# Attention values of the last query tile with V as the stationary operand, in a one-core decoder block kernel

## The chip, the cores and the metric

The kernel runs on one core of one Trainium2 chip. The metric is the device time of one execution in microseconds (us); the time of a version is the median of its runs.

## The reference

One decoder block on x of 512 tokens by 1024 columns, all in float32:

```python
h = rmsnorm(x, ln_mix_g) * (1 + sc1) + sh1
(rq, rk, rv, rg, q, kc, vc, ks, vs, kw, vw, gate) = split(h @ w_in)
y_ret = retention(rope(rq), rope(rk), rv) * silu(rg)          # 4 heads, dk 64, dv 128
y_nsa = g0 * o_cmp + g1 * o_sel + g2 * o_win                  # 8 query heads, 2 groups, dh 64
x = x + ga1 * (concat(y_ret, y_nsa) @ w_out)
h2 = rmsnorm(x, ln_ffn_g) * (1 + sc2) + sh2
x = x + ga2 * ((silu(h2 @ w_gate) * (h2 @ w_up)) @ w_down)
return rmsnorm(x, ln_final_g)
```

With 512 tokens the selected branch takes all 8 blocks and the window covers everything before a query, so `o_sel` and `o_win` are each a causal softmax attention over up to 512 keys: `softmax(mask(q k^T / 8)) v`, with their own keys and values and the same queries. The change touches these two for the last 128 queries.

## The kernel before, in words

Each engine has a program of its own, written out by hand and joined by semaphores: the tensor engine (PE), the vector engine (DVE), the scalar engine (ACT), GpSimd (POOL) and the DMA queue of SyncE (SP). There are four token tiles of 128. Accuracy in the large products is had by splitting both sides into a high and a low part of type fp32r and adding three products; plain float32 products are used where the operands are not split, and PE executes such a product as two records of the profile.

**The attention loop.** A group x is (query tile i, branch b), x = 2i + b, so there are 8 groups; group x has i + 1 key tiles, which gives 20 steps (`STEP0` holds the first step of each group). Groups 6 and 7, steps 12 to 15 and 16 to 19, are the last query tile. Step n consists of

- `scores(n)` on PE: for both head groups g, the transposed scores of one key tile (128 keys on the partitions, 4 heads x 128 queries along the row) into PSUM banks 0 and 1, from four products of 64 rows each (lines 1343, 1345, 1347, 1350), plus the causal mask (line 1341 or 1355) where j = i. It waits until the exponentials of the step before are read out;
- `exp(n)` on ACT (line 610): 128x512 for each head group into `PT[:, n % 2]`, a buffer for two steps;
- `values(n)` on PE (line 1368): 8 plain float32 products, one per head, each with 128 columns of `PT` as the stationary operand and 65 columns of V moving. The 65th column of V is 1, so the sum of the weights falls out beside the output. It waits for exp(n), and it is issued one step late, behind scores(n + 1).

A loop over half steps (`SLOTS`, called slots below) places everything: slot 2n holds scores(n), slot 2n + 1 holds values(n - 1). Tables such as `PAIR_AT`, `RS_AT`, `RV_AT`, `CO_AT`, `M_AT` say behind which half the side work goes on every engine: `pair(x, h)` (line 1317), the raw scores from which DVE takes row minima with `row_min` (line 916); retention scores and values (lines 1411 and 1425), the decay multiply on DVE (line 984), the squares on ACT (line 620), the power on POOL (line 433); compressed attention (line 1400 and DVE line 973); `mix_transposes(i)` (line 1436), the transposes of a finished tile, behind `mix_high` on ACT and `mix_low` on DVE (line 1001).

Before a `pair` of query tile 3 or a retention score PE waits for everything that it issued earlier into banks 4 and 5:

```python
def maxima_free():
    for kind, s_ in (("pair", mx_min), ("block", mb_ok), ("decay", r_dec)):
        if issued[kind]:
            pe.wait_ge(s_, issued[kind])
```

When a group's values are done, DVE divides them by their sums and multiplies by the gate in `add_branch` (lines 935, 936, 939) and adds them to `mix` in `mix_branch` (line 947).

**The output projection.** `out_unit(t, k)` is six 128x512 products (lines 1232 to 1234) of token tile t and 128 rows of w_out, into banks 2t and 2t + 1. After the loop PE does four units (tiles 0 and 2, k = 0, 1), then mix_transposes(3), then twelve more for k < 4. Then it waits for the low parts of w_out rows k = 4 to 7, and does the last 16 units, tile by tile. DVE prepares those rows (scaling, line 849; low part, line 752, with ACT's high part, line 477, between) only after `mix_low(3)` in its program. SP reloads x and then the last w_out unit after the last scores, because x1 lies on the query buffers.

Of the kernel before, what the change touches and what calls it, by code (L numbers as in the profile page):

```python
# [7 lines left out]
F32 = mybir.dt.float32  # L8
# [42 lines left out]
GROUPS = 2 * TT  # L51
STEP0 = [0, 1, 2, 4, 6, 9, 12, 16, 20]
STEPS = STEP0[-1]
PAIR_AT = {1: [(4, 0)], 3: [(4, 1)], 6: [(4, 2)], 7: [(4, 3)], 10: [(5, 0)], 12: [(5, 1)], 13: [(5, 2)], 14: [(5, 3)], 15: [(6, 0)], 16: [(6, 1)], 19: [(6, 2)], 22: [(6, 3)], 24: [(7, 0)], 26: [(7, 1)], 29: [(7, 2)], 30: [(7, 3)]}
MAX_AT = {0: 2, 2: 3, 9: 4, 17: 5, 23: 6, 31: 7}
CS_AT = {9: 2, 21: 3}
CT_AT = {15: 2, 23: 3}
CO_AT = {0: 1, 16: 2, 25: 3}
RS_AT = {8: (1, 0), 11: (1, 1), 18: (2, 0), 21: (2, 1), 27: (3, 0), 28: (3, 1)}
RV_AT = {2: [(0, 0), (0, 1)], 10: [(1, 0)], 13: [(1, 1)], 20: [(2, 0)], 22: [(2, 1)], 29: [(3, 0)], 33: [(3, 1)]}  # L60
SQ_AT = {3: 0, 13: 1, 22: 2, 35: 3}
NORM_AT = {5: 0, 14: 1, 23: 2, 36: 3}
M_AT = {7: 0, 18: 1, 27: 2}
OUT_AT = {16: 0, 18: 1, 27: 2, 34: 3}
SLOTS = 2 * (STEPS + 1)
RAW = 7
EARLY = 8

# [39 lines left out]
def block_kernel(nc, x, c, ln_mix_g, ln_ffn_g, w_ada, b_ada, w_in, cmp_pe_k, cmp_w1_k, cmp_w2_k,  # L108
# [17 lines left out]
    with ExitStack() as ctx:  # L126
# [35 lines left out]
        QTl = at("QTl", [P, HPG, T], F32R, R + 8)  # L162
        KTh = at("KTh", [P, 2, T], F32R, R + 16)
        KTl = at("KTl", [P, 2, T], F32R, R + 20)
        V = at("V", [P, TT, 2, NG, DE], F32, R + 24)
        rqT = at("rqT", [P, 2, T], F32, R + 28.125)
        rkT = at("rkT", [P, 2, T], F32, R + 32.125)
# [17 lines left out]
        tmpo = at("tmpo", [P, T], F32, 107)  # L185
        sqj = at("sqj", [P, T], F32, 109)
        mcol = at("mcol", [P, 2, P], F32, 111)

        wxh = at("wxh", [P, OUT_TAIL, D], F32R, R + 16)
        wxl = at("wxl", [P, OUT_TAIL, D], F32R, R + 32)  # L190
# [25 lines left out]
        expo = small("expo", [P, TT])  # L216
        gates = small("gates", [P, TT, 3 * NH])
        rgt = small("rgt", [P, NH])
        mnc = small("mnc", [P, NH])
        yss = small("yss", [P, RH])  # L220
        hs = small("hs", [P, 2, 2 * CP])
# [121 lines left out]
        def _(sp):  # L343
# [32 lines left out]
            for kind, j in items:  # L376
                if kind == "early":
                    load_early(j)
                    continue
                if (kind, j) == ("w", 2):  # L380
                    sp.dma_start(cst[:, P:K_N], consts[:, P:K_N]).then_inc(const_in, 16)
                if kind == "w" and j in (9, 11):
                    sp.wait_ge(ada_used, ADA_OPS)
                    i = (j - 9) // 2
                    sp.dma_start(w1[:, i, :, :], (cmp_w1_k, cmp_w1_v)[i].rearrange("(j p) n -> p j n", p=P)).then_inc(w1_in, 16)
                if (kind, j) == ("w", 14):
                    sp.dma_start(masks[:, :], consts[:, K_N:K_N + T]).then_inc(masks_in, 16)
                if (kind, j) == ("w", U0_OUT):
                    sp.wait_ge(pairs_ps, 2 * NG)
                    sp.dma_start(decay[:, :, :], decays).then_inc(decay_in, 16)  # L390
                if (kind, j) == ("w", U0_GU + 38):
                    sp.wait_ge(mod_read, 10)
                    sp.dma_start(gfin[:, :], ln_final_g.partition_broadcast(P)).then_inc(gfin_in, 16)
                if (kind, j) == ("w", U0_GU - 1):

                    sp.wait_ge(st_ps, NG * STEPS)
                    sp.wait_ge(cs_ps, TT)
                    for t in range(TT):
                        sp.dma_start(x1[:, t, :], x[t * P:(t + 1) * P, :]).then_inc(xagain_in, 16)
                refill(ring.index((kind, j)))  # L400
# [8 lines left out]
        def _(pool):  # L409
# [31 lines left out]
            pool.dma_start(ga2[:, :], b_ada[5 * D:6 * D].partition_broadcast(P)).then_inc(bias2_in, 16)  # L441
            pool.wait_ge(mod_read, 7)
            pool.memset(mcol[:, :, :], 0.0).then_inc(mcol_set, 1)
            for i in range(TT):
                power(N_RET + i, yss[:, :])
            for u in range(U0_GU, UNITS):
                if u == U0_GU + SPLIT:
                    for t in range(TT):
# [7 lines left out]
        def _(a):  # L456
# [146 lines left out]
            def exp(n):  # L603
                for g in range(NG):
                    a.wait_ge(st_ps, NG * n + g + 1)
                    if n == 1:
                        a.wait_ge(r_y, 2)
                    if n >= 2:
                        a.wait_ge(pv, n - 1)
                    a.activation(PT[:, n % 2, g, :], ps[:, g, :], ACT.Exp, scale=-1.0).then_inc(p_exp, 1)  # L610

            def mix_high(i):
                a.wait_ge(mixT_ps, i + 1)
                a.activation(hTh[:, :, i * P:(i + 1) * P], ps[:, 6:8, :].rearrange("p b (k q) -> p (b k) q", k=4),
                             ACT.Copy).then_inc(mix_hi, 1)

            def ret_squares(i):
                a.wait_ge(r_y, 2 * (i + 1))
# [32 lines left out]
            cmp_copy(1)  # L651

            for n in range(SLOTS):
                if n % 2 == 0 and n // 2 < STEPS:
                    exp(n // 2)
                if n - 1 in CS_AT:
                    cmp_exp(CS_AT[n - 1])
                if n in CT_AT:
                    cmp_copy(CT_AT[n])
                if n in SQ_AT:  # L660
                    ret_squares(SQ_AT[n])
                if n in M_AT:
# [74 lines left out]
        def _(v_):  # L737
# [191 lines left out]
            def add_branch(x):  # L929

                i, b = divmod(x, 2)
                d.wait_ge(pv, STEP0[x + 1])
                o = ps[:, 2:4, 0:HPG * DE].rearrange("p g (h e) -> p g h e", e=DE)
                r = rgt[:, :].rearrange("p (g h) -> p g h", g=NG)
                then(d.reciprocal(r, o[:, :, :, DH]))
                then(d.tensor_tensor(rgt[:, :], rgt[:, :], gates[:, i, (b + 1) * NH:(b + 2) * NH], ALU.mult))
                if x:
                    d.wait_ge(b_mix, x)
                d.tensor_tensor(tmpo[:, :].rearrange("p (g h e) -> p g h e", g=NG, e=DH), o[:, :, :, 0:DH],
                                r.unsqueeze(3).broadcast_to([P, NG, HPG, DH]), ALU.mult).then_inc(o_read, 1)  # L940
            def mix_branch(x):

                i = x // 2
                d.wait_ge(o_read, x + 1)
                d.wait_ge(c_mix, i + 1)
                y = mix[:, i % 2, 512:1024]
                d.tensor_tensor(y, y, tmpo[:, :], ALU.add).then_inc(b_mix, 1)
                d.wait_ge(b_mix, x + 1)
# [125 lines left out]
            row_min(3, 3)  # L1074

            for n in range(SLOTS):
                if n % 2 and n // 2 in STEP0[1:]:
                    add_branch(STEP0.index(n // 2) - 1)
                for x, h in PAIR_AT.get(n, []):
                    row_min(x, h)  # L1080
                if n in MAX_AT:
                    max_rows(MAX_AT[n])
                if n % 2 and n // 2 in STEP0[1:]:
                    mix_branch(STEP0.index(n // 2) - 1)
                if n in CS_AT:
                    cmp_scores(CS_AT[n])
# [13 lines left out]
                    low(U0_OUT + OUT_AT[n - 1])  # L1100
                if n + 1 in OUT_AT:
                    scale_unit(U0_OUT + OUT_AT[n + 1])
            mix_low(TT - 1)

            def residual(t):
# [121 lines left out]
        def _(pe):  # L1227
# [129 lines left out]
            def values(n):  # L1357
# [11 lines left out]
                                 start=j == 0 and h == 0, stop=j == i and h == HPG - 1)  # L1369
                ins.then_inc(pv, 1)  # L1370

            def cmp_scores(i):
                if i == 0:
                    pe.wait_ge(kcT_lo, 1)
# [176 lines left out]
            for n in range(SLOTS):  # L1551
# [1 line left out]
                    scores(n // 2)  # L1553
                    half_rows(n)
                if n % 2 and n >= 3:
                    values(n // 2 - 1)
                if n in MAX_AT:
                    max_transpose(MAX_AT[n])
                if n in CS_AT:
# [23 lines left out]

            wait_low(pe, U0_OUT + 1)
            pe.wait_ge(mix_lo, TT - 1)
            pe.wait_ge(p_exp, NG * STEPS)
            pe.wait_ge(mb_ok, GROUPS)
            for k in range(2):  # L1590
                for t in (0, 2):
                    out_unit(t, k)
            mix_transposes(TT - 1)
            pe.wait_ge(o_read, GROUPS)
            out_unit(1, 0)
            out_unit(1, 1)
            pe.wait_ge(mix_lo, TT)
            for k in range(KT - OUT_TAIL):
                if k >= 2:
                    wait_low(pe, U0_OUT + k)  # L1600
                for t in range(TT) if k >= 2 else (TT - 1,):
                    ins = out_unit(t, k)
                ins.then_inc(unit_used, 1)

            def h2_transposes(t):
                pe.wait_ge(xb_ok, t + 1)
# [130 lines left out]
```

## Time and profile before

| | |
|---|---|
| median of 3 runs | 698.05 us (697.51 to 699.13) |
| profiled execution | 698.45 us, of which the span from first to last instruction is 696.6 us |
| PE busy | 671.5 us, 96% of the span |
| DVE, ACT, POOL busy | 334.2, 227.6, 187.8 us |
| attention steps and side work | about 185 to 279.5 us of the span |
| output projection up to its last 16 units | 279.5 to 302.3 us |

All times in rows are us from the start of the span unless marked ns. PE is busy nearly all the time, so what matters is how much time an instruction holds PE, and where PE would stand still. A matmul record's duration includes its pipeline, so the distance between the starts of two records tells how long one holds the engine.

### The profile page before, as it was taken

What the parts mean: (1) busy time and instruction counts of PE and PEld (TensorE: products, weight loads), DVE (VectorE), ACT (ScalarE), POOL (GpSimd) and SP (SyncE); (2) the same over time, 40 slices, a digit from 0 to 9 for tenths busy, and PEclk for the clock granted to TensorE, in tenths of its full rate; (3) what the DMA queues carried; (4) which work ended last, traced back from release to release, by engine and by line L of the source; (5) the groups of instructions that cost most, each with busy time, mean ns of one, the idle gap of its engine ahead of it and who ended that gap; (6) DMA issues with size and microseconds to landing.
All of it is one profiled execution on the core that took longest, in us unless ns stands there. A gap on an engine that the chain in (4) does not pass through costs nothing.

```text
span 696.6 us, 8985 instructions
## 1 busy us (share of the span) xinstructions
PE 671.5 (96%) x3571; PEld 560.8 (80%) x3571; DVE 334.2 (48%) x574; ACT 227.6 (33%) x384; POOL 187.8 (27%) x95
## 2 busy tenths in 40 slices
PE   2799999999999999999999999999999999999996
PEld 1699889887787878888988888888888888888885
DVE  4888988756577874626312531101000039533126
ACT  4546333250243434236432222222222122332224
POOL 2000000000000001050254445534444338455521
PEclk9899999999999999999999999999999999999998
DMA  9988967530000000870054545433432213231003
GB/s 309 362 277 309 384 226 278 208 121 32 0 2 1 1 1 30 248 206 1 3 158 143 152 144 157 121 91 90 121 118 95 91 60 121 95 111 68 0 1 121
DMA packets 74537, 88.08 MB, mean 126 GB/s; under 512 B 3112, under 2 KB 57600, under 8 KB 74368
## 3 DMA queue, kind: packets, MB, share of 16 engines
q1 hardware_dynamic: 73184, 85.31, 37.7%
q10 hardware_dynamic: 896, 1.12, 0.4%
q0 software_dynamic: 416, 1.08, 0.4%
q8 instruction: 28, 0.46, 0.3%
q14 instruction: 13, 0.11, 0.0%
HBM read 85.41 MB, written 2.10 MB: 126 GB/s over the span
## 4 chain that ended last, share of the span: by engine, by line
PE 93%; DVE 3%; issue 1%; DMA 1%; ACT 1%; SPq 0%; POOL 0%; POOLq 0%; DVEq 0%; ACTq 0%
PE ps L1232 14%; PE ps L1233 14%; PE ps L1234 14%; PE ps L1631 12%; PE ps L1632 12%; PE ps L1630 11%; PE ps L1368 5%; PE ps L1425 1%; PE ps L1317 1%; PE ps L1503 1%; DMA xs<-in_x 1%; PE ps L1343 1%; PE ps L1411 1%; PE ps L1245 1%; DVE acc L767 1%
## 5 line engine op out<-in xcount | busy, mean ns | idle before, releaser
L428 POOL TENSOR_TENSOR wl<-raw,wh 128x1024 fp32r<-128x1024 f32 x66 | 172.3, 2615 | 203.4 <-ACT wh L477 203.3
L1630 PE MATMUL ps<-hTh,wh 128*128 128x512 f32 (+1 forms) x384 | 143.6, 374 | 0.0
L1632 PE MATMUL ps<-hTh,wl 128*128 128x512 f32 (+1 forms) x384 | 142.6, 371 | 0.0
L1631 PE MATMUL ps<-hTl,wh 128*128 128x512 f32 (+1 forms) x384 | 142.6, 371 | 0.0
L477 ACT ACTIVATE wh<-raw 128x1024 fp32r<-128x1024 f32 x94 | 97.0, 1038 | 133.9 <-PE ps L1632 74.0
L1162 DVE TENSOR_TENSOR act<-ps,sg 128x512 f32<-128x512 f32 x22 | 15.2, 692 | 195.1 <-PE ps L1632 195.1
L1232 PE MATMUL ps<-wh,hTh 128*128 128x512 f32 (+2 forms) x232 | 90.2, 389 | 2.5 <-DVE hTl L821 2.5
L1233 PE MATMUL ps<-wl,hTh 128*128 128x512 f32 (+2 forms) x232 | 87.3, 376 | 0.0
L1234 PE MATMUL ps<-wh,hTl 128*128 128x512 f32 (+2 forms) x232 | 87.3, 376 | 0.0
L1630 PEld LDWEIGHTS ps<-hTh,wh 128*128 128x128 f32 x384 | 72.4, 188 | 13.0 <-issue 0.5
L1631 PEld LDWEIGHTS ps<-hTl,wh 128*128 128x128 f32 x384 | 72.4, 188 | 12.9 <-issue 0.5
L1632 PEld LDWEIGHTS ps<-hTh,wl 128*128 128x128 f32 x384 | 72.4, 188 | 12.3
L1232 PE MATMUL ps<-wh,ah 128*128 128x512 f32 x176 | 68.5, 389 | 0.0
L1233 PE MATMUL ps<-wl,ah 128*128 128x512 f32 x176 | 68.5, 389 | 0.0
L1234 PE MATMUL ps<-wh,al 128*128 128x512 f32 x176 | 68.5, 389 | 0.0
L1232 PEld LDWEIGHTS ps<-wh,hTh 128*128 128x128 f32 x232 | 44.4, 191 | 11.1 <-issue 3.1
L1157 DVE TENSOR_TENSOR al<-act,ah 128x512 fp32r<-128x512 f32 x22 | 28.3, 1288 | 50.5 <-ACT ah L701 50.5
L1234 PEld LDWEIGHTS ps<-wh,hTl 128*128 128x128 f32 x232 | 44.2, 191 | 8.0
L1233 PEld LDWEIGHTS ps<-wl,hTh 128*128 128x128 f32 x232 | 44.3, 191 | 7.3 <-issue 0.5
L849 DVE TENSOR_TENSOR raw<-raw,ga 128x1024 f32<-128x1024 f32 x30 | 44.8, 1511 | 0.0
L708 ACT ACTIVATE sg<-ps 128x512 f32<-128x512 f32 x22 | 13.2, 598 | 89.4 <-PE ps L1632 89.4
L433 POOL TENSOR_TENSOR yss<-yss,expo 128x4 f32<-128x4 f32 x4 | 5.0, 1242 | 135.9 <-DVE yss L990 135.9
(194 smaller groups left out, 867.4 us busy)
## 6 DMA issues: line engine op xcount, KB each, us to landing
raw<-in_w_ada SPq DMA_DIRECT2D x32, 512.0 KB, 5.4
raw<-in_w_ff_gate SPq DMA_DIRECT2D x22, 512.0 KB, 4.0
raw<-in_w_ff_up SPq DMA_DIRECT2D x22, 512.0 KB, 3.8
raw<-in_w_ff_down SPq DMA_DIRECT2D x22, 512.0 KB, 3.3
raw<-in_w_in SPq DMA_DIRECT2D x20, 512.0 KB, 7.6
early<-in_w_ada SPq DMA_DIRECT2D x16, 512.0 KB, 10.0
raw<-in_w_out SPq DMA_DIRECT2D x8, 512.0 KB, 3.7
xs<-in_x SPq DMA_DIRECT2D x4, 512.0 KB, 5.7
```

Of the source, the lines that this page charges most:

```text
L428: pool.tensor_tensor(lo, raw[:, slot, 0:n], hi.bitcast(F32), ALU.subtract).then_inc(w_lo2, 1)
L477: a.activation(split(u, n)[0], raw[:, slot, 0:n], ACT.Copy).then_inc(w_hi, 1)
L849: d.tensor_tensor(raw[:, slot, :], raw[:, slot, :], ga[:, :], ALU.mult).then_inc(w_scaled, 1)
L1157: d.tensor_tensor(al[:, f % SPLIT, :], act[:, f, :], ah[:, f % SPLIT, :].bitcast(F32), ALU.subtract).then_inc(a_lo, 1)
L1162: d.tensor_tensor(act[:, f, :], ps[:, 2 * (f % 2) + 1, :], sg[:, f % 2, :], ALU.mult).then_inc(act_ok, 1)
L1232: mm(o, ah_, bh_, start=first, stop=False)
L1233: mm(o, ah_, bl_, start=False, stop=False)
L1234: return mm(o, al_, bh_, start=False, stop=last)
L1368: ins = mm(ps[:, 2 + g, h * DE:(h + 1) * DE], PT[:, n % 2, g, h * P:(h + 1) * P], V[:, j, b, g, :], start=j == 0 and h == 0, stop=j == i a ...
L1630: mm(o, hi[:, ks], hTh[:, k, c0:c1], start=k == 0, stop=False)
L1631: mm(o, hi[:, ks], hTl[:, k, c0:c1], start=False, stop=False)
L1632: ins = mm(o, lo[:, ks], hTh[:, k, c0:c1], start=False, stop=k == KT - 1)
```

## The change

For groups 6 and 7 (steps 12 to 19) `values` is replaced by `wide_values`: V is the stationary operand (64 columns), the 512 weights of one head group move, and the two head groups write the two halves of the partitions of bank 2. The output is transposed (value columns on partitions), and V's column of ones is not used, so the sums of the weights are made apart: POOL adds the weights of a group's four steps in six additions (`weight_sum`), and after the loop PE sums them over the partitions with four products whose stationary operand is one column of ones (`den_sums`), which write partitions 0, 32, 64 and 96 of bank 3. ACT copies outputs and sums out of PSUM, PE transposes them back (8 + 4 transposes), DVE divides and adds (`den_gates`, `add_wide`). ACT's exp(n) now also waits for POOL where POOL still reads the buffer. More of the output projection (all of k < 4 for tiles 0 and 2) is done before mix_transposes(3). Some side work is in other slots. The reload of x waits for `den_sums`.

```diff
-PAIR_AT = {1: [(4, 0)], 3: [(4, 1)], ... 19: [(6, 2)], 22: [(6, 3)], 24: [(7, 0)], 26: [(7, 1)], 29: [(7, 2)], 30: [(7, 3)]}
+PAIR_AT = {1: [(4, 0)], 4: [(4, 1)], ... 20: [(6, 2)], 22: [(6, 3)], 24: [(7, 0)], 25: [(7, 1)], 29: [(7, 2), (7, 3)]}
-RV_AT = {2: [(0, 0), (0, 1)], 10: [(1, 0)], 13: [(1, 1)], 20: [(2, 0)], 22: [(2, 1)], 29: [(3, 0)], 33: [(3, 1)]}
-SQ_AT = {3: 0, 13: 1, 22: 2, 35: 3}
-NORM_AT = {5: 0, 14: 1, 23: 2, 36: 3}
+RV_AT = {2: [(0, 0), (0, 1)], 11: [(1, 0)], 13: [(1, 1)], 20: [(2, 0)], 22: [(2, 1)], 28: [(3, 0)], 34: [(3, 1)]}
+SQ_AT = {3: 0, 13: 1, 22: 2, 37: 3}
+NORM_AT = {5: 0, 14: 1, 23: 2, 38: 3}
+WIDE = GROUPS - 2
+WIDE0 = STEP0[WIDE]
+SUMMED = [n for x in (WIDE, WIDE + 1) for n in range(STEP0[x] + 1, STEP0[x + 1])]
+FILL = 4
...
# SP, before the reload of x
                     sp.wait_ge(cs_ps, TT)
+                    sp.wait_ge(den_ps, 1)
...
# POOL
-            for i in range(TT):
-                power(N_RET + i, yss[:, :])
+            def weight_sum(n):
+                x, j = step(n)
+                acc_ = sums(x % 2)
+                pool.wait_ge(p_exp, NG * (n + 1))
+                if j > 1:
+                    pool.wait_ge(p_sum, sum_count(n) - 1)
+                pool.tensor_tensor(acc_, weights(n - 1) if j == 1 else acc_, weights(n), ALU.add).then_inc(p_sum, 1)
+            for n in range(SLOTS):
+                if n - 1 in SQ_AT:
+                    power(N_RET + SQ_AT[n - 1], yss[:, :])
+                if n % 2 == 0 and n // 2 in SUMMED:
+                    weight_sum(n // 2)
...
# ACT, in exp(n)
+                    if n >= WIDE0 + 2:
+                        a.wait_ge(p_sum, sum_count(n - 2 if n - 2 in SUMMED else n - 1))
...
+            def out_copy(b):
+                a.wait_ge(pv, STEP0[WIDE + b + 1])
+                a.activation(OT[:, b, :], ps[:, 2, :], ACT.Copy).then_inc(oT_ok, 1)
+            def den_copy():
+                a.wait_ge(den_ps, 1)
+                a.wait_ge(r_sq, TT)
+                a.activation(denR[:, :], ps[:, 3, :], ACT.Copy).then_inc(den_ok, 1)
...
             for n in range(SLOTS):
+                if n == 2 * STEP0[WIDE + 1] + 2:
+                    out_copy(0)
...
+            out_copy(1)
+            den_copy()
             mix_high(TT - 1)
...
# DVE, behind the loop, which keeps add_branch and mix_branch for groups 0 to 5
+            den_gates()
+            for b in range(2):
+                add_wide(b)
+                mix_branch(WIDE + b)
             mix_low(TT - 1)
...
# PE
+            def wide_values(n):
+                x, j = step(n)
+                i, b = divmod(x, 2)
+                if j == 0:
+                    if b:
+                        pe.wait_ge(oT_ok, 1)
+                    else:
+                        pe.wait_ge(o_read, WIDE)
+                pe.wait_ge(p_exp, NG * (n + 1))
+                for g in range(NG):
+                    ins = mm(ps[g * DH:(g + 1) * DH, 2, :].rearrange("p (h q) -> p h q", h=HPG), V[:, j, b, g, 0:DH], weights(n)[:, g],
+                             start=j == 0, stop=j == i)
+                ins.then_inc(pv, 1)
+            def den_sums():
+                pe.wait_ge(p_sum, len(SUMMED))
+                for b in range(2):
+                    for g in range(NG):
+                        c = CP * (NG * b + g)
+                        ins = mm(ps[c:c + 1, 3, :].rearrange("p (h q) -> p h q", h=HPG), ones[:, 0:1], sums(b)[:, g], start=True, stop=True)
+                ins.then_inc(den_ps, 1)
...
-            for k in range(2):
+            out_unit(0, 0)
+            out_unit(2, 0)
+            den_sums()
+            out_unit(0, 1)
+            out_transposes(1)
+            den_transposes()
+            out_unit(2, 1)
+            out_transposes(0)
+            for k in range(2, FILL):
                 for t in (0, 2):
                     out_unit(t, k)
             mix_transposes(TT - 1)
             pe.wait_ge(o_read, GROUPS)
-            out_unit(1, 0)
-            out_unit(1, 1)
+            for k in range(FILL):
+                out_unit(1, k)
             pe.wait_ge(mix_lo, TT)
...
+            for k in range(FILL):
+                out_unit(TT - 1, k).then_inc(unit_used, 1)
```

`den_transposes` and `out_transposes(b)` are four 128x128 transposes each (three calls in all, 12 transposes); `den_gates` is a reciprocal and a multiply of 128x16; `add_wide(b)` is one 128x512 multiply out of PSUM, followed by `mix_branch`.

## Rows read from the trace of the kernel before

**Rows 1.** The page: busy time of engines, and the chain that ended last, by engine.

```profile
PE 671.5 (96%) x3571; PEld 560.8 (80%) x3571; DVE 334.2 (48%) x574; ACT 227.6 (33%) x384; POOL 187.8 (27%) x95
PE 93%; DVE 3%; issue 1%; DMA 1%; ACT 1%; SPq 0%; POOL 0%; POOLq 0%; DVEq 0%; ACTq 0%
```

**Rows 2.** Windows: length, busy time (instructions) of PE, PEld, DVE, ACT, POOL; clock, DMA.

```profile
223.00:243.00 20.00, 20.00 (x172) 17.45 (x173) 15.99 (x34) 8.23 (x20) 0.63 (x1) 1.00 0.01 2
243.00:259.00 16.00, 15.51 (x138) 13.05 (x138) 12.72 (x21) 5.56 (x9) 0.38 (x1) 1.00 0.00 1
259.00:279.50 20.50, 20.50 (x162) 17.14 (x160) 9.17 (x18) 7.40 (x19) 1.91 (x1) 1.00 0.12 41
```

**Rows 3.** Timeline of PE, the last steps: start, duration, instruction, count.

```profile
268.22 0.49 PE L1343 MATMUL ps<-QTh,KTh 64*128 64x512 f32 x2
...
269.00 0.39 PE L1350 MATMUL ps<-MB,onesR 64*128 64x512 f32 x2
269.32 2.00 PE L1368 MATMUL ps<-V,PT 128*128 128x65 f32 x16
...
275.42 0.73 PE L1355 MATMUL ps<-identR,maskR 128*128 128x512 f32 x2
275.99 3.68 PE L1368 MATMUL ps<-V,PT 128*128 128x65 f32 x32
279.48 0.48 PE L1232 MATMUL ps<-wh,hTh 128*128 128x512 f32 x1
```

**Rows 4.** The chain: one plain float32 product of 128x512, all columns.

```profile
460.19 0.86 PE ps L1271 x2
```

**Rows 5.** Timeline of PE, slots 26 to 30.

```profile
247.05 0.50 PE L1343 MATMUL ps<-QTh,KTh 64*128 64x512 f32 x2
...
250.25 1.04 PE L1436 MATMUL ps<-cst,mix 128*128 128x128 f32 x8
251.22 1.16 PE L1411 MATMUL ps<-rqT,rkT 64*128 64x128 f32 x16
252.13 0.48 PE L1343 MATMUL ps<-QTh,KTh 64*128 64x512 f32 x2
...
256.73 2.00 PE L1425 MATMUL ps<-rv,hTf 128*128 128x128 f32 x16
258.66 0.50 PE L1317 MATMUL ps<-KTh,QTh 64*128 64x512 f32 x2
```

**Rows 6.** Timeline of DVE, the same stretch.

```profile
248.13 0.69 DVE L973 TENSOR_TENSOR mix<-ps,mnc 128x512 f32<-128x512 f32 x1
...
259.20 0.70 DVE L916 CUSTOM_DVE_ANT_0 ps<-ps,masks 128x512 f32<-128x512 f32 x1 [1.85 <-PE ps L1317]
...
260.47 0.14 DVE L916 DVE_READ_ACCUMULATOR2_ANT mcol<- 128x1 f32 x1
```

**Rows 7.** Timeline of ACT: the two exponentials of step 17.

```profile
269.42 1.08 ACT L610 ACTIVATE PT<-ps 128x512 f32<-128x512 f32 x2 [3.79 <-PE ps L1350]
```

**Rows 8.** POOL: the largest operation (min/median/max ns), by its line.

```profile
L428 POOL TENSOR_TENSOR wl<-raw,wh x66: 2385/2397/3386, 297.7 to 670.5; 128x1024 fp32r<-128x1024 f32 x66
```

**Rows 9.** Timeline of PE, the output projection.

```profile
285.06 1.03 PE L1436 MATMUL ps<-cst,mix 128*128 128x128 f32 x8
285.85 0.48 PE L1232 MATMUL ps<-wh,hTh 128*128 128x512 f32 x1
...
302.26 0.39 PE L1232 MATMUL ps<-wxh,hTh 128*128 128x512 f32 x1
```

**Rows 10.** Timeline of DVE behind the loop.

```profile
288.40 2.35 DVE L849 TENSOR_TENSOR raw<-raw,ga 128x1024 f32<-128x1024 f32 x2
...
295.37 2.50 DVE L752 TENSOR_TENSOR wxl<-raw,wxh 128x1024 fp32r<-128x1024 f32 x2
307.90 1.23 DVE L1108 TENSOR_TENSOR x<-ps,x 128x1024 f32<-128x1024 f32 x1 [10.03 <-PE ps L1234]
```

**Rows 11.** Timeline of the DMA queue SP: the reload of x.

```profile
276.18 1.75 SPq L399 DMA_DIRECT2D x<-in_x  x4
```

More of the change, by code:

```diff
@@ L53 @@
 STEPS = STEP0[-1]
-PAIR_AT = {1: [(4, 0)], 3: [(4, 1)], 6: [(4, 2)], 7: [(4, 3)], 10: [(5, 0)], 12: [(5, 1)], 13: [(5, 2)], 14: [(5, 3)], 15: [(6, 0)], 16: [(6, 1)], 19: [(6, 2)], 22: [(6, 3)], 24: [(7, 0)], 26: [(7, 1)], 29: [(7, 2)], 30: [(7, 3)]}
+PAIR_AT = {1: [(4, 0)], 4: [(4, 1)], 6: [(4, 2)], 7: [(4, 3)], 10: [(5, 0)], 12: [(5, 1)], 13: [(5, 2)], 14: [(5, 3)], 15: [(6, 0)], 16: [(6, 1)], 20: [(6, 2)], 22: [(6, 3)], 24: [(7, 0)], 25: [(7, 1)], 29: [(7, 2), (7, 3)]}
 MAX_AT = {0: 2, 2: 3, 9: 4, 17: 5, 23: 6, 31: 7}
@@ L164, in block_kernel @@
         KTl = at("KTl", [P, 2, T], F32R, R + 20)
+        QTf = at("QTf", [P, 2, HPG, T], F32, R)
         V = at("V", [P, TT, 2, NG, DE], F32, R + 24)
@@ L187, in block_kernel @@
         mcol = at("mcol", [P, 2, P], F32, 111)
+        OT = at("OT", [P, 2, T], F32, 40)
+        denR = sqj
         wxh = at("wxh", [P, OUT_TAIL, D], F32R, R + 16)
@@ L218, in block_kernel @@
         rgt = small("rgt", [P, NH])
+        rgw = small("rgw", [P, 2 * NH])
         mnc = small("mnc", [P, NH])
@@ L232, in ats, with sums, weights @@
             return hTf[:, p, :, (TT - 1) * P:T].rearrange("p (a j) q -> p a j q", a=2)
+        def sums(b):
+            return QTf[:, b].rearrange("p h (t q) -> p t h q", q=P)[:, 0:NG]
+        def weights(n):
+            return PT[:, n % 2].rearrange("p g (h q) -> p g h q", h=HPG)
         rope = cst[:, K_ROPE:K_ROPE + TT * P].rearrange("p (t n) -> p t n", t=TT)
@@ L269, in block_kernel @@
         mx_ps, mx_min, mx_T, mb_ok, st_ps, p_exp, pv, o_read = (sem(n) for n in ("mx_ps", "mx_min", "mx_T", "mb_ok", "st_ps", "p_exp", "pv", "o_read"))
+        p_sum, oT_ok, den_ps, den_ok, denT_ps, den_read, o_T = (sem(n) for n in ("p_sum", "oT_ok", "den_ps", "den_ok", "denT_ps", "den_read", "o_T"))
         c_mix, b_mix, v_ones, mcol_set, masks_in = (sem(n) for n in ("c_mix", "b_mix", "v_ones", "mcol_set", "masks_in"))
@@ L308, in step, with sum_count @@
             return g, n - STEP0[g]
+        def sum_count(n):
+            return SUMMED.index(n) + 1
         def pair_count(g, h):
@@ L940, in add_branch, with den_gates, add_wide @@
                                 r.unsqueeze(3).broadcast_to([P, NG, HPG, DH]), ALU.mult).then_inc(o_read, 1)
+            def den_gates():
+                d.wait_ge(denT_ps, 1)
+                den = ps[:, 3, :].rearrange("p (h c z) -> p c h z", h=HPG, z=CP)[:, :, :, 0]
+                d.reciprocal(rgw[:, :].rearrange("p (c h) -> p c h", h=HPG), den).then_inc(den_read, 1)
+                d.wait_ge(den_read, 1)
+                then(d.tensor_tensor(rgw[:, :], rgw[:, :], gates[:, TT - 1, NH:3 * NH], ALU.mult))
+            def add_wide(b):
+                d.wait_ge(o_T, 2)
+                d.wait_ge(b_mix, WIDE + b)
+                r = rgw[:, b * NH:(b + 1) * NH].rearrange("p (g h) -> p g h", g=NG)
+                d.tensor_tensor(tmpo[:, :].rearrange("p (g h e) -> p g h e", g=NG, e=DH),
+                                ps[:, 3 - b, :].rearrange("p (h g e) -> p g h e", h=HPG, g=NG),
+                                r.unsqueeze(3).broadcast_to([P, NG, HPG, DH]), ALU.mult).then_inc(o_read, 1)
             def mix_branch(x):
@@ L1076, in _ @@
             for n in range(SLOTS):
-                if n % 2 and n // 2 in STEP0[1:]:
+                if n % 2 and n // 2 in STEP0[1:WIDE + 1]:
                     add_branch(STEP0.index(n // 2) - 1)
@@ L1082, in _ @@
                     max_rows(MAX_AT[n])
-                if n % 2 and n // 2 in STEP0[1:]:
+                if n % 2 and n // 2 in STEP0[1:WIDE + 1]:
                     mix_branch(STEP0.index(n // 2) - 1)
@@ L1370, in values, with den_transposes, out_transposes @@
                 ins.then_inc(pv, 1)
+            def wide_values(n):
[18 more added lines that the diff above has]
+                ins.then_inc(den_ps, 1)
+            def den_transposes():
+                pe.wait_ge(den_ok, 1)
+                for h in range(HPG):
+                    ins = pe.transpose(ps[:, 3, h * P:(h + 1) * P], denR[:, h * P:(h + 1) * P], ident)
+                ins.then_inc(denT_ps, 1)
+            def out_transposes(b):
+                pe.wait_ge(oT_ok, 2)
+                if b == 0:
+                    pe.wait_ge(den_read, 1)
+                for h in range(HPG):
+                    ins = pe.transpose(ps[:, 3 - b, h * P:(h + 1) * P], OT[:, b, h * P:(h + 1) * P], ident)
+                ins.then_inc(o_T, 1)
             def cmp_scores(i):
@@ L1555, in _ @@
                 if n % 2 and n >= 3:
-                    values(n // 2 - 1)
+                    (wide_values if n // 2 - 1 >= WIDE0 else values)(n // 2 - 1)
                 if n in MAX_AT:
@@ L1582, in out_unit @@
                 return two_halves(t, U0_OUT + k, (hTh[:, k, tok], hTl[:, k, tok]), k == 0, k == KT - 1)
-            wait_low(pe, U0_OUT + 1)
+            wait_low(pe, U0_OUT + FILL - 1)
             pe.wait_ge(mix_lo, TT - 1)
@@ L1594, in _ @@
             pe.wait_ge(o_read, GROUPS)
-            out_unit(1, 0)
-            out_unit(1, 1)
+            for k in range(FILL):
+                out_unit(1, k)
             pe.wait_ge(mix_lo, TT)
[L1598 to L1603, printed above, removed]
+            for k in range(FILL):
+                out_unit(TT - 1, k).then_inc(unit_used, 1)
             def h2_transposes(t):
```

## The prediction

> **What bounds the kernel now.** I read the page first: PE is busy 96% of the span and makes 93% of the chain [rows 1], so the question is what holds PE, stretch by stretch. The windows over the attention loop say the same of the part that changes: PE is busy 15.51 of 16 us and 20.5 of 20.5 us, at the full granted clock (1.00, its 2.4 GHz level), while POOL does nearly nothing [rows 2]. Then the timelines. In the last steps PE goes from scores to values and back: scores from 268.22, values from 269.32 [rows 3]; ACT's two exponentials take 1.08 us meanwhile and end at 270.50 [rows 7], before the values of the step before end. So ACT is hidden by the values product. The last two values run back to back from 275.99 to 279.48: 1.745 us each [rows 3]. In slots 27 to 30 PE's side work is tied to DVE: a `pair` starts at 258.66, and DVE's `row_min` on it runs from 259.20 to 260.61 [rows 5, 6]. Behind the loop, mix_transposes(3) starts at 285.06 and the last 16 units at 302.26 [rows 9]; DVE's preparation of the last w_out rows ends at 297.87 [rows 10], 4.4 us before PE needs it.
>
> **What a wide product costs.** The stationary side shrinks to 64 columns, the moving side grows to 512. The row for a plain float32 product of 512 columns is 0.86 us [rows 4]. A step has two, one for each half of PE's columns. If the halves run at once a step costs 0.86 us; if one after the other 1.72, which is no gain against 1.745. No row shows two column halves. The nearest rows are products on the two row halves: eight plain float32 products of 128 columns (16 records) hold PE from 251.22 to 252.13, 0.91 us [rows 5], where eight in a row at 0.86/4 would be 1.72. So halves of rows overlap wholly, for this type too, and each pair of scores products does the same. A case between is that only the second record of one product overlaps the first of the next: three records of 0.43, 1.29 us. I take 0.86. Eight steps save 8 x (1.745 - 0.86) = 7.1 us; the other bounds are 3.6 and 0.2.
>
> The rule that speaks against it is in the Trainium skill, "TensorE: Matmul & The Clock Gate", Part 3: a weight load runs beside a product in flight only if the row groups differ. Both wide products use all rows, so by it the second would wait, and the eight steps would save 0.2 us. The same page reports three column tiles 2.38 times as fast as in a row, and "TensorEngine Tiling (Array Packing)", Key Properties, has tiles load and multiply in parallel. No run here shows which holds.
>
> **What is added on PE.** Twelve 128x128 transposes: eight take 0.79 us from 285.06 to 285.85 [rows 9], so 12 take 1.2. `den_sums`: four products of 512 columns on four column groups: 0.86 if all overlap, 2.15 with one record's stagger, 3.44 in a row; I take 0.86 with the case above. The two or three changes of shape amid output units cost about 0.1 each, by the distance from the last scores product to the values (269.00 + 0.23 to 269.32) [rows 3]: 0.3. Together 2.4 us.
>
> **What ends later.** I walk PE forward from slot 25, where the edits first bite; the earlier moved slots change no sum, and PE is busy 20.00 of 20 us there [rows 2], so they can give nothing back.
>
> - Slot 25: pair(7,1) comes ahead on DVE of mix_branch(5) and the compressed output (line 973), which ended at 248.82 [rows 6]. The pair takes the place of scores(13), 247.05 [rows 5]; row_min ends its 0.54 and 1.41 us later, at about 249.05, the two others take 0.7 each: 250.5. mix_transposes(2) needs them. PE arrives at about 249.4: the pair 0.35, scores(13) 1.1, the wide product 0.9. So PE stands 1.1 us, and the transposes start at 250.5, not 250.25 [rows 5]: step 12's whole saving is gone there.
> - Slot 28: ret_values(3,0) now follows the retention scores at once and must wait for mix_low(2): 0.2 us.
> - Slot 29: pair(7,2) and pair(7,3) are adjacent, but `maxima_free` holds the second until row_min of the first is read. From 258.66 to 260.61 is 1.95 us [rows 5, 6], the pair itself takes 0.43: PE stands 1.5 us. What is queued behind it is scores(15), so ACT waits too.
> - POOL: a 128x1024 addition takes 2.4 us, at most 3.4 [rows 8]. exp(14) must wait for the sum of steps 12 and 13. From the start of a scores to the end of its exponentials is 2.28 us (268.22 to 270.50) [rows 3, 7]; exp(13) so ends at 247.4 + 2.28 = 249.7, the sum at 252.2. scores(14) comes after transposes (0.97) and retention scores (0.91) and ends near 253.4. Hidden. exp(18) waits in the same way for the sum of 16 and 17. Walked on with the terms above, scores(17) starts at 265.5, its exponentials end at 267.8, the sum at 270.2, and scores(18) ends at about 270.5. Hidden by 0.3.
> - Steps 16 to 19: with values at 0.86, ACT is no longer hidden. scores takes 1.1, exponentials end 1.08 after they start, and the next scores waits for both. Where no side work is left PE stands some 0.2 to 0.3 us in each of three steps: 0.8.
>
> Sum of these: 3.6, less 0.3 for the present gaps (0.49 us in 243 to 259 [rows 2]): 3.3. The loop would so end 7.1 - 3.3 = 3.8 us earlier, near 275.7.
>
> - Behind the loop: `den_sums` waits for six additions. scores(19) starts near 271.8, so with the mask's 0.57 (275.42 to 275.99) [rows 3] exp(19) ends near 274.6; POOL first finishes step 18's addition, then the power for the retention norm, which now stands ahead of the last addition and takes about 1 us, and ends at about 277.8. Two output units (12 records each at 0.23, that is 1.37 us by 16.41/12 [rows 9]) put PE at 278.4. Hidden, by 0.6. ACT's copies and DVE's divide are hidden by units between (1.37 us against 0.7, 5.5 us against four DVE operations of 0.7).
> - The end of DVE's preparation: it comes behind mix_low(3) and ended 12.81 us after the start of mix_transposes(3) (285.06 to 297.87) [rows 9, 10]. Before, PE had 0.79 + 12 x 1.37 = 17.2 us of work from there. Now four of those units stand ahead of the transposes, and 0.79 + 8 x 1.37 = 11.7 are left. PE stands 1.1 us.
> - SP: x's reload, the last w_out unit and all after it are issued about 3 us later than 276.18 [rows 11]. x is needed at 307.9 [rows 10], 28 us after that. Hidden.
>
> Sum: - 7.1 + 3.3 + 2.4 + 1.1 = - 0.3 us. Against the profiled execution of 698.45 that is 698.15. It is 0.4 above the median of 698.05, so for the median: 697.8.
>
> **Rivals.**
>
> 1. *Column halves in a row.* Nothing shows that they overlap; the overlapping rows are all of row halves. Steps save 0.2, the stand at slot 27 falls to 0.2 and those of steps 16 to 19 vanish (ACT is hidden again), so the idle is 1.9; den_sums 3.44. Sum: - 0.2 + 1.9 - 0.3 + 3.44 + 1.5 + 1.1 = + 7.4: about 705.5. It would decide the sign from about 0.9 us per step on.
> 2. *Overlap of one record only.* - 3.6 + 2.5 + 2.15 + 1.5 + 1.1 = + 3.65: 701.7. Against it: the pairs of records in row halves show no such stagger [rows 5].
> 3. *POOL's additions at 3.4 us, their slowest* [rows 8], since it shares the loop with DVE. The margins of 0.3 and 0.6 are gone: exp(18) 0.7 late, den_sums 1.3 late: + 1.7 over my sum, 699.8. DVE is busy only 9.17 of 20.5 us there [rows 2], so I doubt it.
> 4. *The two stands at slots 27 and 29 are cheaper than walked*, because PE is late there for other reasons. Without their 2.6 us the result is 695.2. For it: my walk adds up DVE latencies from a schedule that will shift. Against it: both orders are fixed in the programs.
>
> **Chances.** Forecast 0.40, rival one 0.18, two 0.12, three 0.06, four 0.24. A measurement of this kernel tells about 0.2% (1.4 us) from no change. The forecast's own range is 696 to 699.5; of it 0.03 is faster, 0.34 the same, 0.03 slower. Faster: 0.24 + 0.03 = 0.27. Same: 0.34 and a little of rival three: 0.36. Slower: 0.37. The range takes in all but rival one: 694.8 to 702.0.
>
> **What the profile after will show.** (1) Wide products: the two of a step start together and a step holds PE 0.86 us; in a row they would be at 1.7. (2) Loop end near 275.7. (3) A gap of about 1.1 us ahead of the transposes near 250 and of 1.5 between two pairs near 258, both ended by DVE. (4) exp(18) not released by POOL. (5) den_sums near 278.4, 0.9 us long, not released by POOL. (6) A gap of about 1 us ahead of the last 16 units, ended by DVE's last low part (line 752). If (1) fails, the sign is settled by that alone; if (1) holds and the result is still off by more than 1.5 us, it is the stands of (3) and (6) that I mis-sized.

## The result

The changed kernel takes 699.11 us (median of 20 runs, 698.26 to 700.52) against 697.75 (20 runs, 697.09 to 699.13): ratio 1.0019, 95% interval 1.0012 to 1.0025, that is 0.8 to 1.7 us slower. I had forecast 0.25 us faster, a change within 0.2%. The loss is small, but clear of the noise.

Its profiled execution took 698.74 us, span 696.9. The page: PE is busy 3.2 us less than [rows 1], POOL 13 us more, and the chain is 89% PE and 5% DVE instead of 93% and 3%.

```profile
PE 668.3 (96%) x3495; PEld 548.7 (79%) x3495; DVE 341.7 (49%) x572; ACT 229.2 (33%) x387; POOL 201.0 (29%) x101
PE 89%; DVE 5%; issue 2%; ACT 2%; DMA 1%; SPq 0%; POOL 0%; POOLq 0%; DVEq 0%; ACTq 0%
```

The windows of the same two stretches as [rows 2]:

```profile
243.00:259.00 16.00, 13.48 (x110) 9.34 (x106) 15.14 (x23) 5.23 (x8) 4.70 (x2) 1.00 0.00 1
259.00:279.50 20.50, 19.39 (x107) 9.63 (x107) 12.07 (x14) 8.53 (x21) 10.51 (x5) 1.00 0.00 1
```

PE now stands idle for 2.5 us of the first 16, and DVE is busy for 15.14 of them (12.72 before): in that stretch DVE has become the bound. The timeline of PE shows where it stands. At the end of a line are the idle time before the instruction and what ended it; such an idle time is called a stand below.

```profile
245.34 1.08 PE L1512 MATMUL ps<-BD,pcT 128*128 128x256 f32 x4
246.35 0.49 PE L1389 MATMUL ps<-KTh,QTh 64*128 64x512 f32 x2
...
247.71 1.08 PE L1455 MATMUL ps<-PT,V 128*64 128x512 f32 x4
249.82 1.06 PE L1548 MATMUL ps<-cst,mix 128*128 128x128 f32 x8 [1.04 <-DVE mix L1041]
...
253.68 1.16 PE L1523 MATMUL ps<-rqT,rkT 64*128 64x128 f32 x16 [0.76 <-DVE hTf L1052]
...
256.76 1.08 PE L1455 MATMUL ps<-PT,V 128*64 128x512 f32 x4
257.77 0.51 PE L1389 MATMUL ps<-KTh,QTh 64*128 64x512 f32 x2
259.78 0.50 PE L1389 MATMUL ps<-KTh,QTh 64*128 64x512 f32 x2 [1.50 <-DVE mcol L967]
...
265.59 0.50 PE L1415 MATMUL ps<-QTh,KTh 64*128 64x512 f32 x2 [0.16 <-ACT PT L646]
...
272.11 0.50 PE L1415 MATMUL ps<-QTh,KTh 64*128 64x512 f32 x2 [0.17 <-ACT PT L646]
...
273.89 2.09 PE L1455 MATMUL ps<-PT,V 128*64 128x512 f32 x8
275.91 0.50 PE L1304 MATMUL ps<-wh,hTh 128*128 128x512 f32 x1
...
278.90 1.04 PE L1465 MATMUL ps<-QTf,ones 128*1 128x512 f32 x8
279.87 0.50 PE L1304 MATMUL ps<-wh,hTh 128*128 128x512 f32 x1
...
289.53 1.03 PE L1548 MATMUL ps<-cst,mix 128*128 128x128 f32 x8
302.40 0.50 PE L1304 MATMUL ps<-wxh,hTh 128*128 128x512 f32 x1 [0.94 <-DVE wxl L803]
```

A wide step (four records) holds PE 1.01 us (256.76 to 257.77): the two column halves overlap. The weight loads (PEld) of all four records come at its start:

```profile
256.76 0.20 PEld L1455 LDWEIGHTS ps<-PT,V 128*64 128x64 f32 x4
```

The four products of `den_sums` (eight records) hold PE 0.97 us: four column groups overlap too. The stands foreseen at slots 27 and 29 and ahead of the last 16 units are there. As foreseen, neither exp(18) nor `den_sums` waits for POOL.

The two profiled executions differ already ahead of the loop, so I compare stretches. The first begins with the compressed products of slot 25, which the timeline of the kernel before has at

```profile
246.04 1.08 PE L1400 MATMUL ps<-BD,pcT 128*128 128x256 f32 x4
```

| us | before | changed | difference | forecast |
|---|---|---|---|---|
| slot 25 to the loop's end | 33.44 | 30.57 | -2.87 | -3.8 |
| loop's end to the last 16 units | 22.78 | 26.49 | +3.71 | +3.5 |
| from there to the end of the span | 394.34 | 394.50 | +0.16 | 0 |
| sum | 450.56 | 451.56 | +1.00 | -0.3 |

The first two rows together, 56.22 us before and 57.06 after, are the measure of the experiments below ("the stretch", first part + second part); a trace resolves tenths there (a second profile of the changed kernel, below, has 57.00), where the medians of the kernel before, in the four sets of runs, lie between 697.75 and 698.44.

### The profile page after: what moved, and what is told of

Read it like the earlier page. It is cut to its first block, busy times and chain, and to the rows that moved or that the text cites. A ratio compares the mean times of both kernels' runs of the same rounds, so it can differ in the third digit from the quotient of the medians.

```text
span 696.9 us, 8845 instructions
## 1 busy us (share of the span) xinstructions
PE 668.3 (96%) x3495; PEld 548.7 (79%) x3495; DVE 341.7 (49%) x572; ACT 229.2 (33%) x387; POOL 201.0 (29%) x101
## 3 DMA queue, kind: packets, MB, share of 16 engines
q0 software_dynamic: 416, 1.08, 0.4%
## 4 chain that ended last, share of the span: by engine, by line
PE 89%; DVE 5%; issue 2%; ACT 2%; DMA 1%; SPq 0%; POOL 0%; POOLq 0%; DVEq 0%; ACTq 0%
PE ps L1304 13%; PE ps L1306 13%; PE ps L1305 13%; PE ps L1748 12%; PE ps L1746 12%; PE ps L1747 11%; PE ps L1440 3%; PE ps L1537 1%; PE ps L1389 1%; PE ps L1615 1%; DMA xs<-in_x 1%; PE ps L1415 1%; PE ps L1455 1%; DVE raw L900 1%; PE ps L1317 1%
## 5 line engine op out<-in xcount | busy, mean ns | idle before, releaser
L900 DVE TENSOR_TENSOR raw<-raw,ga 128x1024 f32<-128x1024 f32 x30 | 47.7, 1610 | 0.0
L1305 PEld LDWEIGHTS ps<-wl,ah 128*128 128x128 f32 x176 | 33.0, 188 | 6.9
```

Of the source, the lines that this page charges most:

```text
L900: d.tensor_tensor(raw[:, slot, :], raw[:, slot, :], ga[:, :], ALU.mult).then_inc(w_scaled, 1)
L1305: mm(o, ah_, bl_, start=False, stop=False)
```

## The experiments

**Pairs back.** The changed kernel, with pair(7,1) and pair(7,3) in the slots that they had in the kernel before:

```diff
-... 24: [(7, 0)], 25: [(7, 1)], 29: [(7, 2), (7, 3)]}
+... 24: [(7, 0)], 26: [(7, 1)], 29: [(7, 2)], 30: [(7, 3)]}
```

> The changed kernel with pair(7,1) back in slot 26 and pair(7,3) back in slot 30. My theory (the side work's new places cost what the wide products save): the stand of 1.10 us ahead of mix_transposes(2) goes, that of 1.58 us between the two pairs shrinks to about 0.6 ahead of the last max_transpose, so the loop ends some 2 us earlier and the time is about 1.2 to 2.0 us under the changed kernel, near 697.4 (ratio to the kernel before 0.999 to 1.000). Rival (the stands are only moved: the chain scores, exponentials, scores or POOL's additions hold PE by then): under 0.5 us gained, ratio 1.001 to 1.002, and PE stands longer ahead of scores(14) to (17).

Measured: ratio 0.9999 (0.9990 to 1.0008). Stretch 29.33 + 26.45: 1.28 us under the changed kernel, at the low end of what I expected. The first stand is gone and the one between pairs became 0.50, but another grew:

```profile
253.14 1.16 PE L1523 MATMUL ps<-rqT,rkT 64*128 64x128 f32 x16 [1.64 <-DVE hTf L1052]
...
261.26 0.33 PE L1395 MATMUL ps<-cst,mcol 128*128 128x128 f32 x1 [0.50 <-DVE mcol L967]
```

**Scaling early.** DVE scales w_out rows 4 and 5 ahead of the divide:

```diff
+            for u in (U0_OUT + SPLIT, U0_OUT + SPLIT + 1):
+                scale_unit(u)
             den_gates()
...
             for u in range(U0_OUT + SPLIT, U0_GU):
-                scale_unit(u)
+                if u > U0_OUT + SPLIT + 1:
+                    scale_unit(u)
```

> The changed kernel with DVE scaling w_out rows 4 and 5 ahead of den_gates, while it has nothing to do. My theory: DVE's preparation ends about 2.4 us earlier against mix_transposes(3), the stand of 0.94 us ahead of the last 16 units goes, and nothing else moves: 0.9 to 1.1 us under the changed kernel, ratio to the kernel before about 1.0005. Rival (the two scalings delay the divide, or x's reload or the last w_out unit is late): no gain or a new stand ahead of mix_transposes(3) or of the last units ended by a DMA.

Measured: 0.9995 (0.9987 to 1.0004). Stretch 30.56 + 25.35: the second part is 1.14 us shorter and no stand is left ahead of the last 16 units. My theory held.

**Halves in a row.**

```diff
-                    ins = mm(ps[g * DH:(g + 1) * DH, 2, :].rearrange(...), V[:, j, b, g, 0:DH], weights(n)[:, g],
+                    ins = mm(ps[0:DH, 2 + g, :].rearrange(...), V[:, j, b, g, 0:DH], weights(n)[:, g],
```

> The changed kernel with both wide products of a step on the same column half (two banks instead of two halves of one), so they cannot overlap; the output of one head group is lost. It tells what the overlap of column halves is worth. If each takes 0.86 us, a step holds PE about 1.87 instead of 1.01 us; ACT is then hidden, so some stands vanish: 5.5 to 6.5 us over the changed kernel, ratio to the kernel before about 1.010. If the halves in the changed kernel did not overlap at all, as a rival reading of its records would have it, the time stays that of the changed kernel (1.002).

Measured: 1.0088 (1.0072 to 1.0103), median 704.71 of four executions. Stretch 35.89 + 26.44, 5.3 us over the changed kernel, a little less than I expected. A wide step now holds PE from 257.32 to 259.18, 1.86 us instead of 1.01. So the column halves do overlap in the changed kernel, and that is worth 0.85 us a step. Part of it is not seen in the time, because stands shrink: the one ahead of the transposes is 0.19 instead of 1.04, and the two for ACT are gone.

```profile
248.25 1.93 PE L1455 MATMUL ps<-PT,V 128*64 128x512 f32 x4
250.37 1.06 PE L1548 MATMUL ps<-cst,mix 128*128 128x128 f32 x8 [0.19 <-DVE mix L1041]
...
257.32 1.93 PE L1455 MATMUL ps<-PT,V 128*64 128x512 f32 x4
259.18 0.50 PE L1389 MATMUL ps<-KTh,QTh 64*128 64x512 f32 x2
```

**No sums on POOL.** `weight_sum` is not called, the waits on `p_sum` are gone, `den_sums` reads a constant.

> The changed kernel without POOL's six additions and without the waits on them; the sums of the weights are replaced by a constant, four products of the same size. My theory: the additions cost PE only through DVE, whose operations beside them take 2.0 to 2.9 us instead of 1.2: the decay multiply of slot 27 comes 0.3 us sooner, ret_values and the last steps a little: 0.3 to 0.6 us under the changed kernel, ratio 1.001 to 1.0015. Rival (the additions hold exp(14), exp(18) or den_sums): 1.5 us or more. Other rival: no difference at all (the slow DVE operations are hidden).

Measured: 1.0006 (0.9997 to 1.0016). Stretch 30.27 + 26.44: 0.35 us under the changed kernel; the stand ahead of the retention scores is 0.49 instead of 0.76. As expected: in the trace of the changed kernel no instruction waits for one of POOL's additions, they act through DVE. Two of the eleven executions, of 763.25 and 2359.85 us, are not in the ratio; nothing here shows what held them.

**Pairs back and no sums on POOL**, both edits together.

> Both pairs back and no additions on POOL (sums replaced by a constant, as before). The first experiment gained 1.24 us of the profile where I expected 2. If POOL's stretching of DVE's scaling ate the rest, the stand of 1.64 us ahead of the second retention scores falls to about 0.5 here and the loop from the compressed products to its end takes 28.0 to 28.3 us instead of 29.3. If it was DVE's order alone, it takes 29.0 or more.

Measured: 0.9977 (0.9966 to 0.9988), six executions. First part 28.17, as expected, against 29.33 with POOL's sums: 1.16 us, and the stand of 1.64 is 0.48. So it was POOL that ate the rest of the first experiment. The timelines of DVE in the changed kernel, of POOL there, and of DVE in this experiment:

```profile
249.49 2.92 DVE L900 TENSOR_TENSOR raw<-raw,ga 128x1024 f32<-128x1024 f32 x1
...
254.88 1.23 DVE L1052 TENSOR_TENSOR hTf<-ps,decay 128x1024 f32<-128x1024 f32 x1 [0.22 <-PE ps L1523]
256.02 2.04 DVE L803 TENSOR_TENSOR wl<-raw,wh 128x1024 fp32r<-128x1024 f32 x1
...
276.40 2.15 DVE L1064 SCALAR_TENSOR_TENSOR mix<-tmpo,rg 128x512 f32<-128x512 f32 x1
```

```profile
248.97 2.34 POOL L473 TENSOR_TENSOR QTf<-PT 128x1024 f32<-128x1024 f32 x1 [6.29 <-ACT PT L646]
254.62 2.36 POOL L473 TENSOR_TENSOR QTf<-QTf,PT 128x1024 f32<-128x1024 f32 x1 [3.30 <-ACT PT L646]
...
275.62 2.38 POOL L473 TENSOR_TENSOR QTf<-QTf,PT 128x1024 f32<-128x1024 f32 x1
```

```profile
248.99 1.22 DVE L896 TENSOR_TENSOR raw<-raw,ga 128x1024 f32<-128x1024 f32 x1
```

In the changed kernel the scaling ends at 252.41, 1.10 us after POOL's addition (251.31); the low part at 258.06, 1.08 after 256.98; the norm's last operation at 278.55, 0.55 after 278.00. Each looks as if it began when POOL's addition ended. The decay multiply at 254.88, with one operand in PSUM, took 1.23 us beside the same addition as the low part.

An even slowing would cost an operation a fixed share of the time that it runs beside an addition. The scaling ran 1.82 us beside one and lost 1.70 (2.92 instead of 1.22). In the kernel with everything together (below) a low part ran only 0.47 us beside one (261.15 to 261.62) and lost 0.33:

```profile
259.25 2.37 POOL L473 TENSOR_TENSOR QTf<-QTf,PT 128x1024 f32<-128x1024 f32 x1 [4.50 <-ACT PT L646]
```

```profile
261.15 1.55 DVE L803 TENSOR_TENSOR wl<-raw,wh 128x1024 fp32r<-128x1024 f32 x1
```

That is 0.93 of the overlap in one case and 0.70 in the other, but 0.12 and 0.14 us less than the overlap: it fits an operation that is held until the addition ends, and not an even slowing.

**The tables alone.** The kernel before with the changed kernel's `PAIR_AT`, `RV_AT`, `SQ_AT` and `NORM_AT`.

> The kernel before with the changed kernel's four tables of places (pairs, retention values, squares, norm) and nothing else of the change. My theory: the two pairs in slot 29 cost 1.5 us by themselves, the rest 0.2 to 0.4 us (the values product of step 12, 1.84 us, hides most of DVE's delay ahead of mix_transposes(2)): 1.5 to 2.0 us over the kernel before, ratio 1.002 to 1.003. Rival (the new places suit PE's order and only the wide products make them look bad): ratio 1.000.

Measured: 1.0045 (1.0027 to 1.0062), median 700.21 against 698.36, so 1.85 us over, as expected. Ten of twelve executions took 699.28 to 702.40 us, two 705.02 and 705.98, and the ratio counts them all. The two have a mean granted clock of 0.984, the ten of 0.989 to 0.994. The one of 705.98 is the profiled one; its windows show where the clock fell:

```profile
255.00:261.00 6.00, 4.50 (x38) 4.10 (x38) 3.76 (x6) 0.00 (x0) 0.00 (x0) 1.00 0.01 3
261.00:263.00 2.00, 2.00 (x12) 1.26 (x11) 1.41 (x4) 0.00 (x0) 0.00 (x0) 0.72 0.00 0
263.00:268.00 5.00, 5.00 (x25) 4.48 (x25) 0.69 (x1) 1.09 (x2) 0.00 (x0) 0.50 0.00 0
268.00:273.00 5.00, 5.00 (x24) 4.23 (x22) 0.34 (x2) 1.08 (x2) 0.00 (x0) 0.50 0.00 0
273.00:279.00 6.00, 6.00 (x42) 5.08 (x42) 3.87 (x5) 2.14 (x3) 0.00 (x0) 0.79 0.01 3
```

**The tables, pairs apart**, and **the double pair only**: the tables with pair(7,3) left in slot 30, and the kernel before with nothing but pair(7,3) moved to slot 29.

> The kernel before with the changed tables except that pair(7,3) stays in slot 30. If the loss of the tables alone (ratio 1.0045 with the fall of the clock in some executions, about 1.0025 without) is the adjacent pairs, this is 1.000 to 1.0006 and shows no stand over 0.5 us and no lower clock. If the rest of the tables (pair(7,1), retention values, squares) carries the loss, 1.001 or more.

> The kernel before with one edit: pair(7,3) moved from slot 30 to slot 29, next to pair(7,2). My theory: 1.5 us of standing and nothing else, ratio 1.002 to 1.0025; and if it is this stand that lets the clock fall, an execution now and then at about 704 to 706 us. Rival (the tables lose in several places): under 1.001.

Measured: 1.0004 (0.9995 to 1.0014), stretch 33.70 + 22.82, and 1.0021 (1.0012 to 1.0030), stretch 34.84 + 22.79. The one misplaced pair carries the tables' loss: 1.41 us of the stretch by itself, 0.30 for all the rest. None of the 11 executions with the double pair alone was above 700.27, so in as many executions this stand by itself did not make the clock fall; that is too few to rule it out.

**Everything together.** Pairs back, scaling early, and w_out row 2 three slots later, so that no long DVE operation meets POOL's first addition:

```diff
-OUT_AT = {16: 0, 18: 1, 27: 2, 34: 3}
+OUT_AT = {16: 0, 18: 1, 30: 2, 34: 3}
```

> The changed kernel with pair(7,1) and pair(7,3) back in their slots, two w_out scalings ahead of den_gates, and the scaling of w_out row 2 moved from slot 26 to slot 29, so that the decay multiply no longer waits for an operation that POOL stretches to 2.9 us. My theory: the gains of the first two experiments add up (1.2 and 1.1 us) and the stand ahead of the retention scores, 1.64 us there, shrinks to about 0.5: 3.4 us under the changed kernel, 2 us under the kernel before, ratio 0.9965 to 0.9975. Rival (the next chain, exponentials or POOL, takes the place): 0.998 to 0.9995.

> The changed kernel unaltered, for the comparison on the same chip: ratio 1.001 to 1.0025 by every theory; from the start of the attention loop on it should lose about 1.0 us of the profile, as in the first pair of traces.

Measured on one chip: everything together 0.9967 (0.9956 to 0.9979), 695.83 us, five executions; the changed kernel 1.0014 (1.0006 to 1.0023), 698.96, stretch 30.55 + 26.45 = 57.00; the kernel before 698.36. Stretch with everything together 28.55 + 25.35 = 53.90, so 3.2 us under the changed kernel and 2.3 under the kernel before. Its timeline of PE:

```profile
247.08 1.08 PE L1458 MATMUL ps<-PT,V 128*64 128x512 f32 x4
248.09 1.09 PE L1551 MATMUL ps<-cst,mix 128*128 128x128 f32 x8
...
251.69 1.16 PE L1526 MATMUL ps<-rqT,rkT 64*128 64x128 f32 x16 [0.48 <-DVE hTf L1052]
...
260.18 0.33 PE L1398 MATMUL ps<-cst,mcol 128*128 128x128 f32 x1 [0.87 <-DVE mcol L967]
...
298.61 0.39 PE L1307 MATMUL ps<-wxh,hTh 128*128 128x512 f32 x1
```

**Row 2 later still**: its key in `OUT_AT` is 32 instead of 30 (DVE scales the row in the slot before its key), for the 0.87 us.

> The best version so far with the scaling of w_out row 2 in slot 31 instead of 29, behind the last row_min, so that it no longer stands ahead of it on DVE. The stand of 0.87 us ahead of the last max_transpose falls to 0.5: 0.3 to 0.4 us under that version, ratio 0.996 to 0.9968. Rival (ACT's high part of row 2, now behind exp(16), or DVE's low part beside POOL's additions delays the last steps): same or slower.

Measured: 0.9973 (0.9965 to 0.9982), stretch 28.89 + 25.36, 0.35 us longer where I expected 0.3 to 0.4 less. The 0.87 became 0.50, but scores(19) now waits 0.87 us for ACT, which was 0.17 before. The lines of PE, ACT, POOL and DVE show the way there:

```profile
271.31 0.50 PE L1418 MATMUL ps<-QTh,KTh 64*128 64x512 f32 x2 [0.87 <-ACT PT L646]
```

```profile
270.18 1.09 ACT L646 ACTIVATE PT<-ps 128x512 f32<-128x512 f32 x2 [1.19 <-POOL QTf L473]
```

```profile
266.96 3.10 POOL L473 TENSOR_TENSOR QTf<-PT 128x1024 f32<-128x1024 f32 x1 [3.79 <-ACT PT L646]
```

```profile
266.60 1.22 DVE L900 TENSOR_TENSOR raw<-raw,ga 128x1024 f32<-128x1024 f32 x1
```

exp(18) waits for POOL's addition of steps 16 and 17, and that took 3.10 us instead of 2.37. It started 0.36 us behind DVE's scaling of row 3, ran 0.86 us beside it and lost 0.73, again the overlap less 0.13; DVE's operation took its 1.22. So here it was POOL that was held. The rival was right that the last steps would be late; the wait that ended last was one for POOL.

## Why the prediction was wrong

The forecast had the sign wrong. It hung on a difference of two sums of 7 us, and the error in it is 1.3 us of the profile. Two steps failed above all: the saving of a wide step was put too high, and the present gaps of the loop were counted as given back, while one of them grew because POOL's additions delay DVE. My own chances already put slower (0.37) ahead of faster (0.27), against the value that I gave. The steps one by one:

- **Overlap of the column halves: right.** In a row they cost 0.85 us a step more. The rule against it, from the Trainium skill, "TensorE: Matmul & The Clock Gate", Part 3 (a weight load runs beside a product only if the row groups differ), does not hold here: both products use all 128 rows. Its figure for three column tiles (faster than in a row) and the sentence of "TensorEngine Tiling (Array Packing)", Key Properties (tiles work in parallel), agree with these 1.01 us.
- **The saving of a step: the term that was mis-sized.** The prediction put 0.86 us against 1.745, "Eight steps save 8 x (1.745 - 0.86) = 7.1 us". The trace has 1.01 for a wide step and 2.02 for the last two: 8.08 for all eight. The old ones, from start to the next instruction's start, took 1.84, 1.84, 1.83, 1.83, 1.93, 1.92 and 3.49 for two: 14.68. So 6.6 us were saved. I took the bare product on both sides, without what entering and leaving it costs: 0.15 us a step for the new ones (1.01 - 0.86), 0.09 for the old (14.68 / 8 - 1.745). 0.5 us of the error.
- **The stands in the loop: places right, sum too small.** The table's first row, -2.87, with the 6.6 saved leaves 3.73, where I had 3.3 net. Slot 27 cost 1.10 (forecast 1.1) and slot 29 1.58 (1.5). The two waits for ACT in the last steps cost 0.47 by the starts (0.8 for three), and `ret_values(3,0)` did not wait at all (0.2). But I had counted 0.3 us of the present gaps as given back, and the stand ahead of the second retention scores, 0.49 before, grew to 0.76 instead: 0.28 us by the starts. Dearer changes of shape around the wide products are left, 0.3, which I had not counted in the loop. What I missed in the grown stand is DVE behind POOL: the decay multiply came late by it, and without POOL's additions the stand is 0.49 again. I had only looked at what waits for POOL (nothing, which was right), not at what POOL's work does to DVE. The Trainium skill, "GPSIMD Engine Reference", Specifications, names contention with DVE instructions that have two SBUF inputs; the rows agree, and the decay multiply with its PSUM operand went free. 0.4 us of the error.
- **Behind the loop: right within 0.2.** den_sums 0.97 (0.86), transposes 1.15 (1.2), the stand ahead of the last 16 units 0.94 (1.1); the rest is 0.65, where I had 0.3 for changes of shape (the first output product behind one takes 0.31 to 0.34 us instead of 0.23).
- **The last 394 us: 0.16 us** for which I had nothing. The nine profiles with the wide steps have 394.42 to 394.78 us there, the four with the old ones 394.31 to 394.40, so a loss of this size is likely real; its cause is open.

These make 1.3 us, with -0.3 forecast and +1.0 found. Rival four (the stands would be cheaper) was wrong; rivals one to three did not occur. (Rival three's 699.8 adds its 1.7 us to the profiled execution's 698.15; on the median's 697.8 it is 699.5.) The side work's new places were the loser: with pairs back alone the stretch is 0.44 us under the kernel before (55.78 against 56.22), and with the two further edits of order the same wide products give 2.3 us.

That POOL's addition holds DVE's operation back until it has ended rests on the ends of such operations in the profiles above; it was not tried by itself.

## What to carry to other kernels

When PE's product gets cheaper, walk the engines that work beside it, and ask of a new operation on one engine what it does to its neighbour: here DVE set four waits on PE, and the edits of order against them turned 0.8 us lost in the stretch into 2.3 gained. When an edit moves work to another time, look again at every pair of operations that now run side by side: row 2's last move cost 0.35 us in that way. Two instructions on PE that another engine must part must not be neighbours: moving one pair by a slot cost 1.4 us. Price an instruction from its start to the next one's start in the same surroundings, not by the bare product, when the sum is near zero.

## What the runs showed of the hardware

- Plain float32 products with 64 columns stationary on the two column halves overlap wholly (1.01 us for two of 0.86), and four with one column stationary on the four groups do too (0.97 us for four), though all use all rows.
- 128x1024 DVE operations with both inputs in SBUF that started during a 128x1024 POOL addition took 2.04 to 2.92 us instead of 1.22 in the changed kernel, and ended 1.08 to 1.10 us after POOL's; POOL's took 2.34 to 2.39 us. A 128x4 TENSOR_SCALAR on DVE (273.12) took 1.43 instead of 0.17. Where DVE's operation had started first (row 2 later still), it took its 1.22 us and the addition 3.10.
- In the profiled execution of the tables alone the granted clock went from 1.00 (2.4 GHz) to 0.50 (1.2 GHz) near 262 us and stayed there to beyond 273, after PE had been busy 4.50 of 6 us, with a stand of 1.50. The stretch was 41.12 + 22.81, 6.3 us over that of the double pair alone. The same stand in the double pair's profile, again 4.50 of 6 us busy, left the clock at 1.00, and so did the changed kernel's. What decides is open.
